# Rounded passes for the pooled branch of a mixer's gates, and the second layer's modulations moved to the end of the first layer

## The reference

```python
# first block, mixer: 1024 positions, 1024 channels
u_pool, q, k, v, o, i_pre, f_pre, ga, gb = split(h @ w_in)
y_a = pool_mixer(u_pool, w_pool, pool_scale) @ w_br_a      # the pooled branch, 512 -> 1024
y_b = (sigmoid(o) * mlstm(...)) @ w_br_b                   # the other branch
merged = sigmoid(ga) * y_a + sigmoid(gb) * y_b
x = x + merged @ w_out                                     # then the experts
...
# second block, layers 0 and 1
c_act = silu(c)
for layer in range(2):
    shift, scale, gate = split(c_act @ w_ada[layer] + b_ada[layer])   # "modulations", 3072 numbers
    h = rmsnorm(x, norm_g[layer]) * (1 + scale) + shift
    ...                                                    # four branches, 16 heads or groups
    x = x + gate * (y @ w_out[layer])
```

## Time and profile before

| | us |
|---|---|
| Time, median of 3 runs (lowest to highest) | 3364.64 (3363.71 to 3365.63) |
| The profiled execution, its own time | 3369.68 |
| its span, first to last instruction | 3367.6 |

### The profile page before, as it was taken

The page is one execution under the profiler, slowest core; times in us unless marked ns, Lnnn a source line. Parts: engine busy times, 40 slices in busy tenths (PEclk is TensorE's granted clock), DMA queues, the critical chain, the costliest instruction groups (busy, mean ns, idle before and its releaser), DMA issues. The chain is left out here.

```text
span 3367.6 us, 55457 instructions
## 1 busy us (share of the span) xinstructions
PE 3313.2 (98%) x23626; PEld 2746.0 (82%) x23626; DVE 2101.0 (62%) x2531; ACT 1602.6 (48%) x1893; POOL 313.2 (9%) x265
## 2 busy tenths in 40 slices
PE   9999999999999998999999999999999999999998
PEld 7887676778888887788888888888788888888887
DVE  7665453459988897756656663555676567753544
ACT  5332111338787875443356543533443356643432
POOL 0000000000111012000123110000000123120000
PEclk9999999999999999999999999999999999999999
DMA  6211442359999997122111111343122111111433
GB/s 230 78 56 54 168 162 76 140 217 396 415 415 415 414 414 297 70 76 88 52 64 52 45 64 51 106 182 125 67 71 83 58 46 58 40 62 51 157 124 112
DMA packets 97243, 492.92 MB, mean 146 GB/s; under 512 B 10920, under 2 KB 11432, under 8 KB 59104
## 3 DMA queue, kind: packets, MB, share of 16 engines
q1 hardware_dynamic: 77216, 417.31, 32.4%
q0 software_dynamic: 14160, 51.55, 4.4%
q10 hardware_dynamic: 5616, 20.45, 1.5%
HBM read 431.43 MB, written 57.84 MB: 145 GB/s over the span
## 5 line engine op out<-in xcount | busy, mean ns | idle before, releaser
L136 PE MATMUL ps<-HH,WS 128*128 128x512 f32 (+1 forms) x2576 | 1027.6, 399 | 4.7 <-DVE WS L1578 2.9
L138 PE MATMUL ps<-HH,WS 128*128 128x512 f32 (+1 forms) x2576 | 1006.2, 391 | 0.0
L137 PE MATMUL ps<-HL,WS 128*128 128x512 f32 (+1 forms) x1936 | 755.7, 390 | 0.0
L136 PEld LDWEIGHTS ps<-HH,WS 128*128 128x128 f32 (+1 forms) x2576 | 483.9, 188 | 112.4 <-DVE WS L1578 6.7
L138 PEld LDWEIGHTS ps<-HH,WS 128*128 128x128 f32 (+1 forms) x2576 | 483.4, 188 | 105.2
L1641 ACT ACTIVATE WA<-ps 128x512 f32<-128x512 f32 x240 | 142.7, 595 | 849.6 <-PE ps L138 814.1
L137 PEld LDWEIGHTS ps<-HL,WS 128*128 128x128 f32 (+1 forms) x1936 | 363.4, 188 | 73.9 <-issue 1.5
L136 PE MATMUL ps<-WAR 128*128 128x512 f32 x768 | 306.8, 399 | 0.9 <-DVE WAR L1372 0.9
L138 PE MATMUL ps<-WAR 128*128 128x512 f32 x768 | 301.1, 392 | 0.0
L1578 DVE TENSOR_TENSOR WS<-RAW,WS 128x1024 fp32r<-128x1024 f32 (+2 forms) x152 | 202.0, 1329 | 111.9 <-ACT WS L1573 111.9
L136 PE MATMUL ps<-WS,HH 128*128 128x256 f32 x896 | 259.4, 289 | 3.8 <-DVE WAR L2616 2.3
(11 more groups left out here) (418 smaller groups left out, 5309.8 us busy)
## 6 DMA issues: line engine op xcount, KB each, us to landing
WR<-in_weu SPq DMA_DIRECT2D x36, 1024.0 KB, 9.0
WR<-in_wed SPq DMA_DIRECT2D x36, 1024.0 KB, 8.6
WR<-in_weg SPq DMA_DIRECT2D x35, 1024.0 KB, 10.3
RAW<-in_wo SPq DMA_DIRECT2D x32, 1024.0 KB, 4.9
WA<-in_wada SPq DMA_DIRECT2D x48, 512.0 KB, 4.5
H<-in_weg SPq DMA_DIRECT2D x23, 1024.0 KB, 10.4
H<-in_weu SPq DMA_DIRECT2D x23, 1024.0 KB, 8.5
H<-in_wed SPq DMA_DIRECT2D x22, 1024.0 KB, 10.2
```

Source lines behind the costliest of these rows:

```text
L136: t.matmul(o, l[0], r[0], start=st, stop=False)
L137: t.matmul(o, l[0], r[1], start=False, stop=False)
L138: return t.matmul(o, l[1], r[0], start=False, stop=sp)
```

## The change

*Pooled branch.* ScalarE now evicts the scaled pooled values rounded into new tiles `yh`, and VectorE writes the rest, rounded, into `yp`. In each gate ScalarE copies the pooled branch's weights rounded into a piece of WS (`br`), VectorE makes their rest, and TensorE makes that branch with `mm3`. The other branch stays in float32.

*Modulations.* The gates keep the 24 quarters and six sums of layer 0 (m = 0 to 3). Those of layer 1 go to units 8 to 11 of layer 0 through a new hook at the end of each step of a unit: quarters two at a time (VectorE, and SyncE's loads three ahead), sums at the places in SUMS.

```diff
@@ pool stage
+                wa.take("yh", gi)
         def scalar_pool(a):
+            def pooled(gi):
+                free(a, wa, "yh", gi)
+                for i in range(2):
+                    a.wait_ge(*at("yp_mm", gi, i))
+                    a.activation(half(tl_rounded("yh", gi), i), ps("yp", gi, i), ACT.Identity, scale=p1("pscale", gi))...
...
         def vector_pool(v):
...
-                    v.wait_ge(*at("yp_mm", gi, i))
-                    v.tensor_scalar(half(tl("yp", gi), i), ps("yp", gi, i), p1("pscale", gi), None, ALU.mult).then_inc(
+                    v.wait_ge(*at("yp_hi", gi, i))
+                    v.scalar_tensor_tensor(out=half(tl_rounded("yp", gi), i), in0=ps("yp", gi, i), scalar=p1("pscale", gi),
+                                           in1=half(tl_rounded("yh", gi), i).bitcast(F32), op0=ALU.mult, op1=ALU.subtract).then_inc(
@@ gates
+        def branch_parts(m):
+            w = WS[:, wss.has["br", m] * 2048:wss.has["br", m] * 2048 + 1024]
+            return w[:, 0:512], w[:, 512:1024]
         def scalar_gates(a, m):
             yield from scalar_pass(a, M, tile_no(f"ga{m}"), ("mg", m), ACT.Sigmoid)
+            free(a, wss, "br", m)
+            a.activation(branch_parts(m)[0], raw(M, source_no(f"ga{m}"))[:, 2048:2560], ACT.Copy).then_inc(*up("br_hi", m))
             yield from scalar_pass(a, M, tile_no(f"gb{m}"), ("gb", m), ACT.Sigmoid)
         def vector_gates(v, m):
...
+            hi, lo = branch_parts(m)
+            v.wait_ge(*at("br_hi", m))
+            v.tensor_tensor(lo, raw(M, source_no(f"ga{m}"))[:, 2048:2560], hi.bitcast(F32), ALU.subtract).then_inc(*up("br_lo", m))
@@ modulations
+        QUARTERS = {**{(8, c): range(22 + 2 * c, 24 + 2 * c) for c in (1, 2, 3)},
+                    **{(U, c): range(6 * U - 24 + 2 * c, 6 * U - 22 + 2 * c) for U in (9, 10, 11) for c in (0, 1, 2)}}
+        SUMS = {(9, 0): (6,), (10, 0): (7, 8), (11, 0): (9,), (11, 3): (10, 11)}
         def quarters(m):
-            return range(8 * m, 8 * m + 8) if m < 6 else ()
+            return range(8 * m, 8 * m + 8) if m < 3 else ()
+        def sums_of(m):
+            return range(2 * m - 2, 2 * m) if 0 < m < 4 else ()
+        def ahead_of(x):
+            return x + AHEAD if x + AHEAD < (24 if x < 24 else 48) else None
+        def sync_quarter(s, x):
+            n, q = x // 4, x % 4
+            free(s, wa, "wq", x)
+            if x >= AHEAD:
+                s.wait_ge(*at("mod_acc", (x - AHEAD) // 4, (x - AHEAD) % 4 * 2 + 1))
+            s.dma_start(tl("wq", x), d["wada"][n // 6, n % 6][:, q * 1024:(q + 1) * 1024])...
+        def sync_modulations(s, U, c):
+            if (U, c) == (8, 0):
+                for x in range(24, 24 + AHEAD):
+                    sync_quarter(s, x)
+            sync_quarters(s, QUARTERS.get((U, c), ()))      # for each x: sync_quarter(ahead_of(x))
+        def tensor_modulations(t, U, c):
+            tensor_sums(t, SUMS.get((U, c), ()))            # waits mod_acc of n, four matmuls
+        def vector_sums(v, ns):
+            for n in ns:
+                v.wait_ge(*at("mod_mm", n))
+                v.tensor_tensor(md[:, 4 * j:4 * j + 4], ps("mod", n)[:, 0:4], p2(layer, "b_ada", 4 * j, 4), ALU.add)...
+        def vector_modulations(v, U, c):
+            vector_sums(v, SUMS.get((U, c), ()))
+            for x in QUARTERS.get((U, c), ()):
+                vector_quarter(v, x)
         def tensor_branches(t, m):
-            w = raw(M, source_no(f"ga{m}"))[:, 2048:3072]
-            for j, nm in ((0, "yp"), (1, "og")):
...
+            w = raw(M, source_no(f"ga{m}"))[:, 2560:3072]
+            hi, lo = branch_parts(m)
+            t.wait_ge(*at("br_lo", m))
+            for i in range(2):
+                free(t, banks, "br", m, 0, i)
+                for k in range(4):
+                    if m == 0:
+                        t.wait_ge(*at("yp", k, i))
+                    ks = slice(k * 128, (k + 1) * 128)
+                    o = mm3(t, ps("br", m, 0, i), (hi[:, ks], lo[:, ks]),
+                            (half(tl_rounded("yh", k), i), half(tl_rounded("yp", k), i)), k == 0, k == 3)
+                o.then_inc(*up("br_mm", m, 0, i))
...
+            tensor_sums(t, sums_of(m))
@@ units, last in each step c of every unit
+                    modulations(e, U, c)
```

More of the change, by code:

```diff
@@ L3231, in scalar_pool @@
         def scalar_pool(a):
-            for gi in range(4):
-                yield from scalar_pass(a, M, tile_no(f"u{gi}"), ("u", gi))
-            yield from scalar_gates(a, 0)
+            def pooled(gi):
+                free(a, wa, "yh", gi)
+                for i in range(2):
+                    a.wait_ge(*at("yp_mm", gi, i))
+                    a.activation(half(tl_rounded("yh", gi), i), ps("yp", gi, i), ACT.Identity, scale=p1("pscale", gi)).then_inc(
+                        *up("yp_hi", gi, i))
+            for gi in range(4):
+                steps = scalar_pass(a, M, tile_no(f"u{gi}"), ("u", gi))
+                next(steps)
+                yield
+                next(steps)
+                if gi:
+                    pooled(gi - 1)
+                yield
+                next(steps, None)
+            gates = scalar_gates(a, 0)
+            next(gates)
+            yield
+            next(gates)
+            yield
+            next(gates)
+            pooled(3)
+            yield
+            yield from gates
         def vector_pool(v):
@@ new lines, in sync_quarters, with tensor_sums @@
+        def sync_quarters(s, xs):
+            for x in xs:
+                if ahead_of(x):
+                    sync_quarter(s, ahead_of(x))
+        def sync_modulations(s, U, c):
+            if (U, c) == (8, 0):
+                for x in range(24, 24 + AHEAD):
+                    sync_quarter(s, x)
+            sync_quarters(s, QUARTERS.get((U, c), ()))
+        def tensor_sums(t, ns):
+            for n in ns:
+                free(t, banks, "mod", n)
+                t.wait_ge(*at("mod_acc", n, 7))
+                for q in range(4):
+                    o = t.matmul(ps("mod", n)[:, q:q + 1], half(tl("acc", n // 2), n % 2)[:, q * 128:(q + 1) * 128], ones[:, 0:1],
+                                 start=True, stop=True)
+                o.then_inc(*up("mod_mm", n))
@@ L3340, in plan_branches @@
                 raws.take("raw", M, x + 2)
[L3341 to L3344, removed]
+            plan_sums(sums_of(m))
             if m == 0:
@@ L3347, in plan_branches @@
                     wa.take("wq", x)
[L3348 to L3353, removed]
-        def sync_branches(s, m):
[L3356 to L3362, removed]
+            plan_quarters(quarters(m))
+        def sync_branches(s, m):
             if m == 0:
                 for x in range(AHEAD):
-                    quarter(x)
+                    sync_quarter(s, x)
             x = source_no(f"ga{m}")
@@ L4345, in units @@
         def units(name, e, layer, squares=lambda e, U: None, between=lambda e, U: None, norm=lambda e, U, n: None,
-                  finish=lambda e, U: None, ahead=lambda e, layer, k: None):
+                  finish=lambda e, U: None, ahead=lambda e, layer, k: None, modulations=lambda e, U, c: None):
             U0 = layer * 12
@@ L4705, in layer_sync @@
             sync_input(s, layer, 1)
-            units("sync", s, layer, finish=sync_finish)
+            units("sync", s, layer, finish=sync_finish, modulations=sync_modulations)
             output_sync(s, layer)
         def layer_tensor(t, layer):
-            units("tensor", t, layer, between=tensor_between, norm=tensor_norm)
+            units("tensor", t, layer, between=tensor_between, norm=tensor_norm, modulations=tensor_modulations)
             output_tensor(t, layer)
@@ L4721, in layer_vector @@
                 vector_input(v, 0, 0)
-            units("vector", v, layer, vector_squares, finish=vector_finish, ahead=vector_out_ahead)
+            units("vector", v, layer, vector_squares, finish=vector_finish, ahead=vector_out_ahead,
+                  modulations=vector_modulations)
             output_vector(v, layer)
```

81 lines of the change are left out of this document (45 added, 36 removed).

## The result

The changed kernel takes 3378.25 us (median of six runs, 3376.8 to 3380.0) against 3364.18 us before (3361.5 to 3368.2): a ratio of 1.0042, 95% interval 1.0032 to 1.0052, that is 14.1 us more, between 10.8 and 17.5.

The account below looks back on a forecast made before the run. The prediction took TensorE, busy 98% of the span, as the bound. Its terms, -11.4 - 5.1 + 2.6 + 3.3 + 20.8 + 4.0 = +14.2 us, gave 3378.8 us on the median's scale, range 3361 to 3389.

Parts of the forecast that it names:

- pooled branch, 8 gates: Gates: each pooled half goes from 16 float32 records (6.86 us) to 24 rounded passes (5.44 us), -11.4 us in all.
- six sums out of the gates: Gates: two sums take TensorE 1.71 us; six sums leave, -5.1 us.
- sums 6 to 8 in units 9 and 10: Units 9 and 10: three of the moved sums come back between TensorE's passes, +2.6 us.
- unit 10's late split: Unit 10: VectorE waits at two bias additions, splits the next weights late, TensorE idles, +3.3 us (0 to 4.8).
- unit 11, scores to first product: Unit 11: row loads queue behind quarter 47; product 31.5 us after scores instead of 10.7, +20.8 us (15.7 to 24.4).
- clock: Unit 11: one drop of TensorE to half clock after idle stretches, +4.0 us (0 to 8).
- the cover of the splits: Gates: added ScalarE copy and VectorE subtraction hide behind the 10.9 us gb pass, costing nothing; otherwise 11 us in all.
- R1: Last units: quarters and sums cost only their TensorE time; -11.4 us, 3353.2 us; chance 0.11.
- R2: Unit 11: first rows land 3.0 us after issue and the clock holds; +5.1 us, 3369.7 us; chance 0.15.
- R3: Unit 11: worst landing of the rows and two full clock drops; +21.8 us, 3386.4 us; chance 0.05.
- R4: Gates: the new passes take 0.429 us like float32 records; +38.8 us against the forecast, 3417.6 us; chance 0.02.

Follow-up runs that it names:

- the moves alone: Changed kernel's moves of quarters and sums, with the branches left in float32 as before the change: 3387.35 us, ratio 1.0075 to before.
- the pooled branch alone: Only the pooled branch in rounded passes; all quarters and sums stay in the gates, two quarter tiles in flight instead of three: 3359.14 us, ratio 0.9987 to before.
- the run with the added matmuls: Changed kernel plus matmuls of constants on TensorE ahead of each of the last two sums in unit 11: 3386.29 us, ratio 1.0065 to before.
- the run with the loads first: Changed kernel with loads of quarters 44 to 47 issued after quarter 41, ahead of the output's loads: 3366.41 us, ratio 1.0008 to before.
- twelve quarters: Pooled branch in rounded passes, all 48 quarters in the first four gates, twelve each, three tiles in flight: 3369.63 us, ratio 1.0016 to before.

## Why the prediction was right

The forecast was 3378.8 us, the measured median is 3378.25. The mechanism came as told, but that the numbers lie so close is luck: the terms of units 10 and 11 were too small, the gain of the sums too, and the measured terms add up to 2.3 us more than the medians show, which is inside their interval. Point by point, "measured" from the rows above:

| Step | Forecast, us | Measured, us |
|---|---|---|
| pooled branch, 8 gates | -11.4 | -11.4 (312.94 - 324.38) |
| six sums out of the gates | -5.1 | -6.0 (324.38 - 330.35) |
| sums 6 to 8 in units 9 and 10 | +2.6 | +2.5 (scores of unit 8 26.4 us earlier, transpose of unit 10 23.9 us earlier) |
| unit 10's late split | +3.3 | +4.6, of it 2.6 idle time and 1.6 by the clock |
| unit 11, scores to first product | +20.8 | +25.2, of it 2.3 by the clock |
| clock | +4.0 | +1.5 in the output passes (2.3 and 1.6 are in the two rows above) |
| sum | +14.2 | +16.4; the medians say +14.1 (10.8 to 17.5) |

**Gates.** Right in the passes; the cover of the splits held, at 0.08 us of idle time. The sums gave 0.9 more than forecast: from branch to branch a gate with two sums lasts 37.34 us and one without 35.51 (the moves alone), 1.83 a pair and not 1.71, and 0.5 lies in the first gate (36.02 before, 35.50), which has none; that part stays open. The Trainium skill (FP8 and Floating Point Precision, TensorE Precision Notes) says that true float32 takes four passes through the array. A float32 matmul here is two records of 0.429 us, 3.8 times the 0.227 of a rounded pass, which agrees nearly. Three rounded passes in place of one float32 matmul are the whole gain here, and it comes in full where VectorE is in time. The two experiments in which it was not show that the cover is thin: in the pooled branch alone, waits of VectorE for single quarters (3.14 us the one shown) were enough to lose 3.5 of the 11.4 us.

**Unit 10.** The mechanism was right, bias additions that hold up VectorE's queue, and putting the sums one step later removes all of it. The idle time was smaller than forecast, 2.6 us; that the clock would fall behind it was not in the sum, and in the moves alone it did not fall.

**Unit 11.** The chain came as told, each link within 1.3 us up to the rows: sum 9's addition at 3.9 us after the scores (forecast 4.0), quarter 45 done at 10.5 (11.8), SyncE's first row at 9.6 (9.9). Then the rows were used at 20.2, not 18.0, and all that is behind is 2.2 later: root 25.4 (23.2), finish 28.2 (26.0), quarters 31.3 (29.2). The term that was too small is the queue ahead of the first rows, and it was the bytes more than the rate. I counted 2.88 MB from quarter 47 on, at 415 GB/s. Quarter 46 was left out: by the prediction's own steps it is issued when quarter 43 is accumulated, so it is still on its way when 47 is issued. In the trace it is issued at 2159.6, 1.2 us ahead of 47, and lands 4.8 us later. From the issue of 47 to the landing of the first row the table has 341 GB/s over 11.9 us, that is 4.1 MB; 0.52 of the 1.2 MB over my count are quarter 46, and the rest is by estimate the rows behind the first, of which three more are issued within 2.3 us and land 10.2 to 10.7 us after their issue, as the first does. At the forecast's own rate and its 2.4 us, 4.1 MB would take an estimated 12.2 us, near the 11.9 measured; 2.88 MB at 341 GB/s would take 10.8. From 2168 to 2170 the table has 410 GB/s, close to the rate I took. The Trainium skill (DMA: Bandwidth & Descriptors, Specifications) has 358 GB/s for one core; by that the rows would have come at an estimated 19.1. That is nearer to what happened, but it is no limit of this core, which moves 410 GB/s there and 412 GB/s from 2192 to 2200.

One wait I hadn't seen: sum 10 stood 8.51 us not for its quarters but for a PSUM bank, which the root of unit 10 reads. It cost nothing, because the root was what the rest waited for anyway.

**Clock.** Sum 11 is followed by the norm sum after 1.70 us instead of 0.81 at full clock (2195.77 to 2196.58 in the run with the added matmuls), and the product follows the norm sum after 2.77 us instead of 1.39: 2.3 us, as that run has it too. From the first product (5.9 us behind the kernel before) to the norm sum behind the output (2286.97 against 2279.57, 7.4 behind) another 1.5. So unit 11 and the output lost 3.8 us by the clock, where the sum has 4.0 for one drop, and unit 10 lost 1.6 that the sum does not have. The 4.0 rested on a reading that is a little short: with a mean of 0.80 in its last window the half clock ends nearer 751.4 than 751.2.

**Rivals.** R1 would have needed the product within 15 us of the scores, and it came at 35.9. R2's condition, rows that land about 3 us after issue, is true where nothing is queued ahead of them (3.2 us in the run with the loads first) and false here (10.5). R3 came nearest in its parts: without the 2.3 of the clock unit 11 cost 22.9 us, under R3's 24.4, and unit 11 and the output lost 3.8 us by the clock, under its 8. R4 is out: the passes are at 0.227 us. Not shown is what each of VectorE's quarters in unit 11 costs by itself; only the 13.8 us left with the loads first, which go to 1.4 when the quarters go and the sums stand elsewhere. Of these 12.4 us 2.3 are the clock, and some 10 are VectorE's quarters with the sums that wait for them.

## What to carry to other kernels

Work that is moved takes its queue entries with it. The six quarters in unit 11 cost twice: the load of the last of them, issued only after a result of that unit, stood ahead of the next stage's loads on SyncE (11.4 us), and on VectorE the quarters stood ahead of what TensorE waited for (some 10 us). Where there is slack is a question for each queue: the same 24 quarters spread over units 8 to 10, with the sums at the second step of a unit, cost only the TensorE time of the six sums, and the gain of the passes stayed (13.2 us, 7 to 16). An engine that is busy for 62% of the span can still be late by one to three microseconds at the one split that TensorE wants next, and half clock can come on top of the idle time (1.6 us in unit 10).

## What the runs showed of the hardware

The granted clock of TensorE was at half for some 3 us behind an idle stretch of 2.60 us (unit 10 of the changed kernel) and one of 2.97 us (gate 1 with twelve quarters). It stayed full behind 1.43 us (gate 1 with two tiles in flight), and also behind 2.59 us at the same place of unit 10 in the moves alone. It was at half for 3.4 us, too, where TensorE had no idle time in the 9 us ahead (378.9 and 457.4 with twelve quarters). So in these runs the length of one idle stretch does not decide it. A 256 KB row load landed 3.2 us after its issue with nothing ahead of it and 10.5 us with the last quarters and two weight loads of 1 MB ahead, while the core moved 341 GB/s.
